# Expert rows added into one DRAM accumulator by the scatters, and the last norm taken beside the last down product

## The reference, cut to what matters

```python
h = layer_norm(DEEPNORM_ALPHA * h + mixed @ w_out[l], ln_mix_g[l], ln_mix_b[l])
ffn = moe_ffn(h, ...)
h = layer_norm(DEEPNORM_ALPHA * h + ffn, ln_ffn_g[l], ln_ffn_b[l])

# moe_ffn, per (token, expert) pair of the top 4, gates = softmax over the 4:
gu = xb @ w_gate_up[e] + b_gate_up[e]
gate, up = minimum(gu[:, :1024], 7), clip(gu[:, 1024:], -7, 7)
y = ((up + 1) * gate * sigmoid(1.702 * gate)) @ w_down[e] + b_down[e]
out = segment_sum(y * slot_gate, token)
```

## Time and profile before

| what | value |
|---|---|
| median of three runs | 1929.81 us (1926.93 to 1930.73) |
| profiled execution | 1928.25 us |
| its span, first to last instruction | 1926.6 us |
| mean granted TensorE clock | 0.973 of full speed |
| PE / DVE / ACT / POOL busy | 95% / 72% / 56% / 14% of the span |
| DMA, read and written in DRAM | 483.29 MB, 23.86 MB |

### The profile page before, as it was taken

How to read it: one execution, slowest core, us unless ns; L and a number is a source line. 1 busy time by engine, 2 the same in 40 slices (tenths; PEclk the granted TensorE clock), 3 DMA queues, 4 the chain that set the end, 5 groups by cost and what they waited for, 6 DMA issues and landing times.

```text
span 1926.6 us, 25983 instructions
## 1 busy us (share of the span) xinstructions
PE 1830.2 (95%) x9168; PEld 1505.0 (78%) x9169; DVE 1387.5 (72%) x1373; ACT 1081.2 (56%) x857; POOL 274.9 (14%) x253
## 2 busy tenths in 40 slices
PE   4999999999999868999999999999999999999984
PEld 4997897778888856888888888888888888888862
DVE  6224523332434467999999999999999999999965
ACT  2423323454412145777777777777777777777750
POOL 2000000000000011212212212212212212212200
PEclk9999999999999878999999999999999999999997
DMA  8322122212231367999999999999999999999945
GB/s 263 96 88 66 56 76 66 66 44 88 88 108 68 136 244 268 342 366 370 353 368 370 351 368 369 350 374 368 353 375 366 356 373 373 344 378 366 351 160 223
DMA packets 139842, 490.59 MB, mean 255 GB/s; under 512 B 20097, under 2 KB 65537, under 8 KB 106514
## 3 DMA queue, kind: packets, MB, share of 16 engines
q1 hardware_dynamic: 119168, 461.40, 64.4%
q0 software_dynamic: 16336, 26.78, 3.9%
q10 hardware_dynamic: 4290, 1.73, 0.4%
HBM read 483.29 MB, written 23.86 MB: 263 GB/s over the span
## 4 chain that ended last, share of the span: by engine, by line
PE 91%; DVE 5%; DMA 1%; issue 1%; ACT 1%; ACTq 0%; DVEq 0%; POOLq 0%
PE psA L1240 21%; PE psA L1242 20%; PE psA L1241 20%; PE psX L1240 6%; PE psX L1241 6%; PE psX L1242 6%; PE psX L1247 4%; DVE wlo L1028 1%; PE psX L1393 1%; PE psX L1379 1%; PE psX L1352 1%; PE psX L1510 1%; PE psA L1445 1%; PE psA L1491 1%; PE psX L1462 1%
## 5 line engine op out<-in xcount | busy, mean ns | idle before, releaser
L1028 DVE TENSOR_TENSOR wlo<-raw,whi 128x2048 fp32r<-128x2048 f32 x384 | 859.7, 2284 | 36.8 <-ACT whi L772 36.7
L772 ACT CAST whi<-raw 128x2048 fp32r<-128x2048 f32 x384 | 727.6, 1911 | 231.7 <-PE psA L1242 218.3
L1240 PE MATMUL psA<-whi,xT_hi 128*128 128x512 f32 x1024 | 407.0, 397 | 2.4 <-issue 2.4
L1242 PE MATMUL psA<-whi,xT_lo 128*128 128x512 f32 x1024 | 400.4, 391 | 0.0
L1241 PE MATMUL psA<-wlo,xT_hi 128*128 128x512 f32 x1024 | 400.3, 391 | 0.0
L1240 PEld LDWEIGHTS psA<-whi,xT_hi 128*128 128x128 f32 x1024 | 193.5, 189 | 41.3 <-issue 2.8
L1242 PEld LDWEIGHTS psA<-whi,xT_lo 128*128 128x128 f32 x1024 | 193.0, 189 | 41.6
L1241 PEld LDWEIGHTS psA<-wlo,xT_hi 128*128 128x128 f32 x1024 | 193.6, 189 | 38.4
L1240 PE MATMUL psX<-whi,aT_hi 128*128 128x512 f32 x512 | 202.7, 396 | 5.8 <-DVE aT_lo L1121 5.8
L1242 PE MATMUL psX<-whi,aT_lo 128*128 128x512 f32 x512 | 200.0, 391 | 0.0
L1241 PE MATMUL psX<-wlo,aT_hi 128*128 128x512 f32 x512 | 200.0, 391 | 0.0
(11 more groups left out here) (288 smaller groups left out, 2394.2 us busy)
## 6 DMA issues: line engine op xcount, KB each, us to landing
raw<-in_w_gate_up SPq DMA_DIRECT2D x256, 1024.0 KB, 7.3
raw<-in_w_down SPq DMA_DIRECT2D x128, 1024.0 KB, 7.1
raw<-in_w_in SPq DMA_DIRECT2D x32, 1024.0 KB, 5.5
yrows<-y_dram SPq DMA_DIRECT2D x4, 2048.0 KB, 14.6
raw<-in_w_gla_proj SPq DMA_DIRECT2D x4, 1024.0 KB, 5.1
raw<-in_w_fox_proj SPq DMA_DIRECT2D x4, 1024.0 KB, 5.1
raw<-in_w_out SPq DMA_DIRECT2D x4, 1024.0 KB, 5.1
xt<-in_x SPq DMA_DIRECT2D x4, 512.0 KB, 8.3
```

The source lines that it names most:

```text
L772: s_.copy(xsplit(c)[0], xraw(slot)).then_inc(hi_ready, 1)
L1028: v.tensor_tensor(lo, xraw(slot), hi.bitcast(F32), ALU.subtract).then_inc(lo_ready, 1)
L1240: mm(dst, sh, mh, start=first, stop=False)
L1242: return mm(dst, sl, mh, start=False, stop=last)
```

## The change

- y_dram with its 2048 rows goes. A new DRAM tensor acc_dram has one row per token (512) and 128 spare rows. Behind the stores of h2 into h2_dram, POOL stores h2 into acc_dram as well, and one tile more into the spare rows.
- `scatter` adds (compute_op add) the rows of y_t to the rows of acc_dram. `didx` is now the token's row, and for a slot without a token the spare row of its partition, so that all 128 rows move each time. Before each scatter POOL waits for the one before it.
- The gates are divided by ALPHA as well, so that acc_dram holds h2 plus the sum over ALPHA; the last norm, of what is now 1/ALPHA of the old rows, uses epsilon over ALPHA squared. The separate destination numbers (`destcode`, `hot[:, 1]`, `dval`) go.
- When the scatter of expert 30 has landed, SP loads the four tiles of acc_dram (`finish`), DVE takes the norm of all rows (`final_norm`) and SP stores them. In program order on every engine but PE this stands ahead of the result of expert 31's down product.
- The rows of expert 31 are gathered from acc_dram into xg; DVE adds the down product, scaled by its gates, straight from PSUM, takes a norm of these rows alone, and POOL scatters them into the output once the four tiles have been stored.
- The adding up behind the experts (load of y_dram, identity matmuls, two additions per tile) goes. With an overflow, which these inputs don't have, expert 31's rows are scattered too and the whole norm is taken again.

```diff
--- before
+++ after
@@ -166,7 +166,6 @@
-    dval = at("dval", 126.5, [P, TT, E])
@@ -201,7 +200,7 @@
-    yrows = at("yrows", 0, [P, TT, TOPK * D])
+    acc = at("acc", 80, [P, TT, D])
@@ -259,7 +261,7 @@
-    y_dram = nc.dram_tensor("y_dram", [T * TOPK, D], F32, kind="Internal").ap()
+    acc_dram = nc.dram_tensor("acc_dram", [T + P, D], F32, kind="Internal").ap()
@@ -429,6 +432,18 @@
+        def finish(n):
+
+            for t in range(TT):
+                sp.dma_start(acc[:, t, :], acc_tiles[t]).then_inc(acc_in[t], 16)
+            for t in range(TT):
+                sp.wait_ge(fin_ready, TT * n + t + 1)
+                sp.dma_start(out_tiles[t], acc[:, t, :]).then_inc(fin_out, 16)
+            sp.wait_ge(fin_out, 16 * TT * (n + 1))
+
+        sp.wait_ge(y_out, 16 * (E - 1))
+        finish(0)
+
@@ -440,20 +455,16 @@
-
-        sp.wait_ge(fin_ready, 1)
-        for t in range(TT):
-            sp.dma_start(yrows[:, t, :], y_tiles[t]).then_inc(yrows_in[t], 16)
-        for t in range(TT):
-            sp.wait_ge(fin_ready, t + 2)
-            sp.dma_start(out_tiles[t], h2[:, t, :]).then_inc(fin_out, 16)
-        sp.wait_ge(fin_out, 16 * TT)
+            sp.wait_ge(over_done, 1)
+            sp.wait_ge(last_out, 16)
+            finish(1)
+        g.memset(eps_f, EPS / ALPHA ** 2).then_inc(eps_ready, 1)
@@ -469,8 +480,7 @@
-        marks.mark(g.iota(destcode, [[TOPK * P, TT], [1, TOPK]], base=-int(BIG), channel_multiplier=TOPK,
-                          allow_small_or_imprecise_dtypes=True))
+        marks.mark(g.iota(spare, [[0, 1]], base=T, channel_multiplier=1, allow_small_or_imprecise_dtypes=True))
@@ -521,7 +531,11 @@
-        token_bound, row_bound = pool.to_reg(T - 1), pool.to_reg(T * TOPK - 1)
+        for t in range(TT):
+            g.dma_start(acc_tiles[t], h2[:, t, :]).then_inc(acc_out, 16)
+        g.dma_start(acc_tiles[TT], h2[:, 0, :]).then_inc(acc_out, 16)
+
+        token_bound, row_bound = pool.to_reg(T - 1), pool.to_reg(T + P - 1)
@@ -535,9 +549,13 @@
+            if isinstance(i, int) and i == 0:
+                pool.wait_ge(acc_out, 16 * (TT + 1))
+            else:
+                pool.wait_ge(y_out, 16 * i)
-            g.indirect_dma_start(y_dram, bass.IndirectOffsetOnAxis(ap=didx[:, 0:1], axis=0), y_t[:], None,
-                                 bounds_check=row_bound, oob_is_err=False).then_inc(y_out, 16)
+            g.indirect_dma_start(acc_dram, bass.IndirectOffsetOnAxis(ap=didx[:, 0:1], axis=0), y_t[:], None,
+                                 bounds_check=row_bound, oob_is_err=True, compute_op=ALU.add).then_inc(y_out, 16)
@@ -567,12 +585,26 @@
-        with pool.Fori(1, E - 1) as i:
+        body(1, False)
+        with pool.Fori(2, E - 1) as i:
-        scatter(E - 1)
+
+        pool.wait_ge(tab_ready, E + 3)
+        pool.wait_ge(y_out, 16 * (E - 1))
+        pool.wait_ge(xt_done, E)
+        pool.sem_inc(gathers, 1)
+        g.indirect_dma_start(xg[:], None, acc_dram, bass.IndirectOffsetOnAxis(ap=didx[:, 0:1], axis=0),
+                             bounds_check=row_bound, oob_is_err=True).then_inc(last_in, 16)
+        pool.wait_ge(last_ready, 1)
+        pool.wait_ge(fin_out, 16 * TT)
+        pool.sem_inc(scatters, 1)
+        g.indirect_dma_start(out[0], bass.IndirectOffsetOnAxis(ap=didx[:, 0:1], axis=0), up_t[:], None,
+                             bounds_check=token_bound, oob_is_err=False).then_inc(last_out, 16)
+        pool.wait_ge(last_out, 16)
+            scatter(E - 1)
@@ -605,7 +637,11 @@
-        act.wait_ge(eps_ready, 1)
+        def final_std(n, t):
+            act.wait_ge(var_ready, n + 1)
+            s_.activation(rstd[:, t:t + 1], mv[:, t, 1:2], ACT.Sqrt, bias=eps_f).then_inc(std_ready, 1)
+
+        act.wait_ge(eps_ready, 2)
@@ -822,6 +858,10 @@
+        for t in range(TT):
+            final_std(2 * TT + t, t)
+        act.wait_ge(var_ready, 3 * TT + 1)
+        s_.activation(lstd, lmean[:, 1:2], ACT.Sqrt, bias=eps_f).then_inc(std_ready, 1)
@@ -835,8 +875,8 @@
-        for t in range(TT):
-            std(2 * TT + t)
+            for t in range(TT):
+                final_std(3 * TT + 1 + t, t)
@@ -1051,7 +1091,7 @@
-            seq.mark(v.tensor_scalar(gates[:, t, :], gate_e[:, t, :], gate_r[:, t:t + 1], 1.0 / SLOPE, ALU.mult,
+            seq.mark(v.tensor_scalar(gates[:, t, :], gate_e[:, t, :], gate_r[:, t:t + 1], 1.0 / (SLOPE * ALPHA), ALU.mult,
@@ -1059,13 +1099,10 @@
-        seq.mark(v.tensor_tensor(hot[:, 1], hot[:, 0], destcode.unsqueeze(2).broadcast_to(shape), ALU.mult))
-        seq.link(v.tensor_reduce(dval[:], hot[:, 1], AX_X, ALU.add))
-        seq.mark(v.tensor_copy(vals[:, :, 0:E, 1], dval[:]))
@@ -1098,8 +1135,8 @@
-            chain.link(v.tensor_copy(queue[:, 3, 0:1], psD[:, 0, 1:2]))
-            chain.mark(v.tensor_scalar(didx[:], queue[:, 0, 0:1], BIG, None, ALU.add))
+            chain.link(v.tensor_copy(queue[:, 3, 0:1], psD[:, 0, 0:1]))
+            chain.mark(v.tensor_scalar(didx[:], queue[:, 0, 0:1], BIG, spare, ALU.add, ALU.min))
@@ -1181,7 +1218,31 @@
-        v.tensor_scalar(didx[:], queue[:, 0, 0:1], BIG, None, ALU.add).then_inc(tab_ready, 1)
+        v.tensor_scalar(didx[:], queue[:, 0, 0:1], BIG, spare, ALU.add, ALU.min).then_inc(tab_ready, 1)
+
+        def final_norm(first, base, fin):
+
+            for t in range(TT + 1):
+                if t < TT:
+                    dve.wait_ge(acc_in[t], first)
+                    norm_stats(t, acc[:, t, :], fin)
+                if t >= 1:
+                    norm_apply(base + t - 1, t - 1, acc[:, t - 1, :], lnffn_g[:], lnffn_b[:], fin).then_inc(fin_ready, 1)
+
+        dve.wait_ge(lnffn_in, 32)
+        fin = Steps(dve, fin_seq, 0)
+        final_norm(16, 2 * TT, fin)
+        dve.wait_ge(last_in, 16)
+        dve.wait_ge(dn_done, E)
+        row = up_t[:]
+        fin.link(v.scalar_tensor_tensor(row, psD.rearrange("p b c -> p (b c)"), queue[:, 0, 1:2], xg[:], ALU.mult, ALU.add))
+        fin.mark(v.bn_stats(lsum[:, 0:6], row[:, 0:512]))
+        fin.link(v.bn_stats(lsum[:, 6:12], row[:, 512:1024]))
+        v.bn_aggr(lmean, lsum).then_inc(var_ready, 1)
+        dve.wait_ge(std_ready, 3 * TT + 1)
+        fin.link(v.reciprocal(lstd, lstd))
+        fin.link(v.scalar_tensor_tensor(row, row, lmean[:, 0:1], lnffn_g[:], ALU.subtract, ALU.mult))
+        v.scalar_tensor_tensor(row, row, lstd, lnffn_b[:], ALU.mult, ALU.add).then_inc(last_ready, 1)
@@ -1193,8 +1254,8 @@
-                chain.link(v.tensor_copy(queue[:, 0, 0:1], psD[:, 0, 1:2]))
-                v.tensor_scalar(didx[:], queue[:, 0, 0:1], BIG, None, ALU.add)
+                chain.link(v.tensor_copy(queue[:, 0, 0:1], psD[:, 0, 0:1]))
+                v.tensor_scalar(didx[:], queue[:, 0, 0:1], BIG, spare, ALU.add, ALU.min)
@@ -1206,28 +1267,9 @@
+            dve.sem_inc(over_done, 1)
+            final_norm(32, 3 * TT + 1, fin)
-
-
-        dve.wait_ge(y_out, 16 * E)
-        dve.wait_ge(dn_done, E)
-        v.tensor_copy(smax, smax).then_inc(fin_ready, 1)
-        dve.wait_ge(lnffn_in, 32)
-        fin = Steps(dve, fin_seq, 0)
-        for t in range(TT):
-            dve.wait_ge(yrows_in[t], 16)
-            row = h2[:, t, :]
-            y = yrows[:, t, :].rearrange("p (k d) -> p k d", k=TOPK)
-            fin.link(v.scalar_tensor_tensor(row, row, ALPHA, y[:, 0, :], ALU.mult, ALU.add))
-            if t >= 1:
-                norm_apply(2 * TT + t - 1, t - 1, h2[:, t - 1, :], lnffn_g[:], lnffn_b[:], fin).then_inc(fin_ready, 1)
-            dve.wait_ge(rest_done, t + 1)
-            rest = psA[:, 2 * (t % 2):2 * (t % 2) + 2, :].rearrange("p b c -> p (b c)")
-            v.tensor_tensor(row, row, rest, ALU.add).then_inc(rest_added, 1)
-            dve.wait_ge(rest_added, t + 1)
-            norm_stats(t, row, fin)
-        t = TT - 1
-        norm_apply(2 * TT + t, t, h2[:, t, :], lnffn_g[:], lnffn_b[:], fin).then_inc(fin_ready, 1)
@@ -1581,16 +1623,6 @@
-        for t in range(TT):
-            pe.wait_ge(yrows_in[t], 16)
-            if t >= 2:
-                pe.wait_ge(rest_added, t - 1)
-            for n in range(2):
-                for k in range(1, TOPK):
-                    ins = mm(psA[:, 2 * (t % 2) + n, :], ident[:], yrows[:, t, k * D + n * 512:k * D + (n + 1) * 512],
-                             start=k == 1, stop=k == TOPK - 1)
-            ins.then_inc(rest_done, 1)
-
```

More of the change, by code:

```diff
@@ L247, in build @@
     tokcode = vec(TT)
-    destcode = vec(TT, TOPK)
+    spare = vec(1)
+    lsum, lmean = vec(12), vec(2)
+    lstd = vec(1)
+    eps_f = vec(1)
     queue = vec(4, 2)
@@ L314, in build @@
     bgu_in, bdn_in = S("bgu_in"), S("bdn_in")
-    yrows_in = [S(f"yrows_in{t}") for t in range(TT)]
-    fin_ready, fin_out, rest_done, rest_added = S("fin_ready"), S("fin_out"), S("rest_done"), S("rest_added")
+    acc_in = [S(f"acc_in{t}") for t in range(TT)]
+    acc_out, last_in, last_ready, last_out = S("acc_out"), S("last_in"), S("last_ready"), S("last_out")
```

(3 more changed lines are left out.)

## The result

The changed kernel takes 1904.83 us, the median of four runs (1902.3 to 1905.31), against 1930.27 for the kernel before on the same chip. The ratio is 0.9864, with a 95% interval from 0.9852 to 0.9877. In a second series it came to 1904.13, ratio 0.9875 (0.9858 to 0.9891). The whole 95% interval lies under 1, so this is a gain of 1.4% clear of the noise. I had forecast 1900.5, in a range of 1895 to 1925. The profiled execution took 1902.3 us with a span of 1900.7, where the one before had 1926.6.

What follows compares the result with a forecast made beforehand. TensorE was taken to bound the loop, so the gain lay in the 49.6 us behind the last product: span 1926.6 - 26.9 (tail) - 1.5 (routing) = 1898.2, time put at 1900.5 us, range 1895 to 1925.

Steps and rivals of the forecast that it cites:

- the signs that the prediction named for being right: Last down product about 1875, last norm's statistics before it, no DVE idling in loop, period 36.1 us, row-wise scatter last.
- Step 1: Tail: expert 30's adding scatter, started at 1860.55, lands at 1868.0; 5.4 us plus 2, bounds 5.4 and 20.
- Step 2: Tail: SP's first load of the sums, 4.2 us with 0.2 to issue, done at 1872.4.
- Step 3: Tail: norm of all rows on DVE, 4 tiles of 4.18 us, 16.7 in all, covering expert 31's down product.
- step 4: Tail: expert 31's rows added from PSUM and normed like today's last tile, 5.94 us, done at 1895.1.
- Step 5: Tail: POOL's row-wise scatter to the output, 4.1 us to land, 0.5 for the last branch, ending at 1899.7.
- The routing: Before the first gather: a multiply, a reduce and a cast leave DVE, 1.5 us gained, bounds 0 and 1.6.
- The accumulator's first stores: Before the first gather: five stores, 2.6 MB, some 6 us, free in POOL's 31.5 us of idling.
- The constants: At the start: put at 0 together with other small additions, bounds -0.1 and +0.3 us.
- the room at 3.8 us per expert: Loop: with the added bytes at 433 GB/s the DMA engines need 32.3 of 36.1 us, so no loss.
- rival B: Loop: DMA engines already full (share 0.97, ceiling 367 GB/s), 2.0 us lost per expert, 1961 us; chance 0.05.
- Rival A: Loop: adding scatter slow as an operation, loss from 17.7 us of landing on, 1977 us at 20; chance 0.11.

Runs made afterwards that it cites:

- e1: The changed kernel with its scatter writing the 128 rows instead of adding them: 1901.95 us, ratio 0.9859.
- e2: The changed kernel without the spare rows, slots without a token being skipped by scatter and gather: 1903.11 us, ratio 0.9874.
- e5: The changed kernel, but SP loads the sums only when expert 31's down product is done, so no overlap: 1914.78 us, ratio 0.9926.
- e4: The changed kernel, but SP instead of POOL waits for the last scatter to land, and POOL loads the overflow count earlier: 1900.53 us, ratio 0.985.
- e3: The changed kernel, but SP stores expert 31's normed rows by a plain DMA at fixed rows, instead of POOL's row-wise scatter: 1898.14 us, ratio 0.9846.
- e12: The changed kernel with the old kernel's three routing instructions put back on DVE, into a column nobody reads: 1907.32 us, ratio 0.989.
- e7: The changed kernel with every adding scatter made twice, the second into an accumulator nobody reads, DVE waiting for both: 1963.13 us, ratio 1.0188.
- e6: The changed kernel without expert 31's own norm: all 32 experts' rows are scattered and added, then one norm: 1912.78 us, ratio 0.991.
- e8: The changed kernel with three adding scatters for each expert: 2179.43 us, ratio 1.1301.
- e9: The changed kernel with two adding scatters per expert but without the spare rows, about 64 rows each: 1952.91 us, ratio 1.0107.

## Why the prediction was right, and where not

The sign and the place held, and so did the mechanism: the load, the identity matmuls and two additions per tile are gone, the norm runs beside the down product, and the loop costs nothing. All the signs that the prediction named for being right were there. The size held less well than it looks: 25.4 us measured by the medians, 29 forecast, and span by span 1898.2 forecast and 1900.7 in the trace, but that is one term 6.1 us too small against several that together were 3.6 us too pessimistic. The steps:

- Step 1, the scatter of expert 30: 7.4 us taken, 6.3 measured, inside the bounds. Adding is 2.9 us in the tail (e1), and fewer rows bring nothing (e2). That I was near is partly luck, for two things that I had not looked at cancel: the 5.4 us that I started from held 3.7 us until the first row moved and 1.3 us for 53 rows, the new scatter 2.2 us and 3.75. The reason I gave, bytes at 433 GB/s, is not what makes the rows slow.
- Step 2, the loads: 4.4 taken, 3.2 measured. Steps 1 and 2 together were 2.3 us too dear.
- Step 3, 16.7 us forecast and 16.4 measured; step 4, 5.94 and 6.0. The down product was covered, with 8.5 us to spare, and e5 shows the 10 us that the cover is worth.
- Step 5 was the term that was mis-sized: 4.1 us to land, measured 4.2, and then "0.5 for the last branch", measured 6.6, 5.4 of them POOL's drain. The trace of before had a hint of it, a drain of 5.6 us that was over 41 us ahead of the end, in its records but in none of the lists that I had read. I had asked what the new last DMA costs and not what its engine does behind it. e4 and e3 show it.
- The routing: 1.5 forecast, 1.4 measured from end to end of its stretch, and 1.5 in e12.
- Another 1.4 us came from ahead of the routing, where nothing was changed but the constants at the start; it is within what that stretch varies between executions, so this part is chance. From the first gather to expert 30's scatter 0.2 us were lost (1170.5 for 1170.3).
- The accumulator's first stores were free: POOL issued them from 664.5 to 667.1 and then idled for 20.3 us. The constants cost 0.1 us at most (PE's first product at 13.58 for 13.46).

The loop cost nothing, as forecast, but with less to spare than I gave. I had put the room at 3.8 us per expert, from 433 GB/s, and 2.2 us of idle DVE behind a landing of 15.5. e7 shows that room for one more adding scatter (2.6 us) was not there: 1.5 us of it came out in the period. The mean share of 98.5% was the better guide, the one that rival B rested on: there were some 0.5 us left by the share, 1.1 by e7. The rate of 433 GB/s is no measure of it. In the fuller slices of the changed kernel's period where weights alone move, the loop itself reaches 418 to 449 GB/s; in the three where most of the added rows move (slices 28 to 30, from 1324.4 on) it has 281, 241 and 245, with the engines as busy. So a scatter is to be counted here in engine time, not in bytes. Nor had the weight loads the slack that I gave them, 18 us less two conversions: in e7 they land in 12 and ScalarE waits. Rival A, the landing, was never near: even with two scatters DVE waited once, for the one that POOL issued in 10.4 us.

The Trainium skill's rule of the two sources, in "Collectives: The Full Stack" (section "The bandwidth ceiling: the fold count and why AG ≠ RS ≠ AR"), agrees with what the packets show: 328 ns for an added row against 159 for a written one, a factor of 2.06. That two reads are the reason, no run here shows. The Trainium skill's figure of about 358 GB/s, in "DMA: Bandwidth & Descriptors" (section "Where 436 GB/s comes from"), is not the ceiling in this kernel, which moved 371 in the loop, but it was nearer to what the loop could take than my 433.

## What to carry to other kernels

When a change moves the last DMA of a program to POOL, look for POOL's drain behind it (5.4 us here) among the records of the trace, and let POOL's last instruction be its issue, with another engine waiting for the landing. A row added by a scatter took twice a written one's time in its packets here, so ask whether the DMA engines have that room in the period, by their share, perhaps by the fullest of them, and not by the best rate seen elsewhere. And take the plain part first: two thirds of the gain (16.4 of 25 us, the shorter routing included) came from adding in DRAM instead of loading four rows per token back, the overlap was the rest.

## What the runs showed of the hardware that was not expected

- POOL ends a program with a drain: 5.4 us from its own start in the changed kernel, where it starts behind the last landing. Started at the last DMA's issue it ended 3.2 us behind the landing (e4), 2.7 where the last DMA landed late (e3, e6). With two scatters per expert it took 8.0 us, with three 1.5. What sets its length is open.
- A row of 4 KB added by an indirect DMA takes 328 ns in its packet and 159 ns written; POOL issues such a scatter of 128 rows in 3.75 us for 3.15 in the loop.
- A third adding DMA of 128 rows issued within 4.4 us of the first held POOL for 12.6 us in 29 of 31 experts (e8), the second for 10.3 us on a few occasions (once in e7, six times in e9).
- A scatter with fewer rows lands hardly sooner (12.0 for 12.6 us in the loop), and fewer packets are in flight at once: 10 for 53 rows, 20 for 128.
